# Query norms ahead of unit edges, weight parts behind the first scores, an early Ln/Exp set, and one masked matrix in place of two

## The reference

```
# GLA, chunks of 64 tokens, both directions (second one on flipped tokens), 4 heads, DK=128, DV=256
att = where(lower_tri, q_dec @ k_inv.T, 0)            # 64 x 64 per chunk
o   = att @ v + q_dec @ s
s   = exp(total)[:, None] * s + k_end.T @ v
out = rms_norm(o_fwd + o_bwd) * silu(r)

# attention: 8 query heads, 2 key/value heads, HEAD_DIM=128; layer 0 with context queries, layer 1 without
q, k = rms_norm(q) * g_q, rms_norm(k) * g_k           # rope on latent tokens only
ctx queries read ctx keys (256); latent queries read all keys (512)
o = softmax(q @ k.T / sqrt(128)) @ v

# RG-LRU input: depthwise conv of 4 taps on p[9], evaluated as the projection leaves the accumulators
```

## Time and profile before

| | us |
|---|---|
| median of 3 runs | 2046.06 (2041.23 to 2046.12) |
| profiled execution, its own time | 2039.92 |
| its span | 2038.2 |
| TensorE busy | 1945.4 (95%) |
| VectorE busy | 1164.4 (57%) |
| ScalarE busy | 1002.7 (49%) |
| mean granted TensorE clock | 0.985 of full |
| HBM traffic | 242.21 MB read, 119 GB/s |

### The profile page before, as it was taken

How to read it: one execution, slowest core, us unless ns; L and a number is a source line. 1 busy time by engine, 2 the same in 40 slices (tenths; PEclk the granted TensorE clock), 3 DMA queues, 4 the chain that set the end, 5 groups by cost and what they waited for, 6 DMA issues and landing times.

```text
span 2038.2 us, 26205 instructions
## 1 busy us (share of the span) xinstructions
PE 1945.4 (95%) x10784; PEld 1578.9 (77%) x10784; DVE 1164.4 (57%) x1622; ACT 1002.7 (49%) x1413; POOL 24.3 (1%) x57
## 2 busy tenths in 40 slices
PE   5999999999999999899999999799898999989998
PEld 3788777777777768577766787688687888989997
DVE  3565445545555334765555433766555678668874
ACT  4533346545654223543333333644355688566663
POOL 2000000000000000000000000000000000000000
PEclk9999999999999999899999999899999999999999
DMA  8211111122233554145454533121222354545553
GB/s 310 66 55 53 57 55 60 62 78 93 93 95 103 186 183 148 52 135 199 163 198 163 176 104 106 52 73 55 75 84 72 125 161 147 173 145 166 185 180 122
DMA packets 67990, 244.96 MB, mean 120 GB/s; under 512 B 7696, under 2 KB 8736, under 8 KB 67872
## 3 DMA queue, kind: packets, MB, share of 16 engines
q1 hardware_dynamic: 64736, 232.81, 34.6%
q0 software_dynamic: 1696, 5.24, 0.8%
q10 hardware_dynamic: 1440, 5.24, 0.7%
HBM read 242.21 MB, written 1.05 MB: 119 GB/s over the span
## 4 chain that ended last, share of the span: by engine, by line
PE 73%; DVE 15%; ACT 5%; DMA 3%; issue 3%; SPq 0%; ACTq 0%; DVEq 0%
PE ps L1454 52%; PE ps L1444 4%; DVE wlo L833 4%; PE ps L1389 3%; DVE fa L862 2%; DMA wada<-in_w_ada 2%; ACT whi L438 2%; PE ps L1489 2%; PE ps L1706 2%; PE ps L1796 2%; PE ps L1727 1%; DVE state L1177 1%; DMA wraw<-in_weights 1%; PE ps L1620 1%; PE ps L1630 1%
## 5 line engine op out<-in xcount | busy, mean ns | idle before, releaser
L833 DVE TENSOR_TENSOR wlo<-wraw,whi 128x1024 fp32r<-128x1024 f32 x352 | 429.5, 1223 | 403.4 <-ACT whi L438 402.5
L438 ACT ACTIVATE whi<-wraw 128x1024 fp32r<-128x1024 f32 x352 | 371.4, 1056 | 377.9 <-PE ps L1454 193.7
L1454 PE MATMUL ps<-hh,whi 128*128 128x512 f32 (+1 forms) x1664 | 381.2, 351 | 1.9 <-ACT l_ti L772 1.8
L1454 PE MATMUL ps<-hl,whi 128*128 128x512 f32 (+1 forms) x1664 | 375.0, 348 | 0.0
L1454 PE MATMUL ps<-hh,wlo 128*128 128x512 f32 (+1 forms) x1664 | 344.0, 348 | 1.9 <-DVE wlo L833 1.9
L1454 PEld LDWEIGHTS ps<-hh,whi 128*128 128x128 f32 x1664 | 274.5, 191 | 58.7 <-issue 22.6
L1454 PEld LDWEIGHTS ps<-hl,whi 128*128 128x128 f32 x1664 | 277.1, 191 | 40.2 <-issue 3.6
L1454 PEld LDWEIGHTS ps<-hh,wlo 128*128 128x128 f32 x1664 | 269.6, 190 | 40.4 <-issue 3.0
L862 DVE SCALAR_TENSOR_TENSOR fa<-ps,par,fa 128x510 f32<-128x510 f32 (+1 forms) x176 | 100.1, 610 | 27.8 <-ACT fa L516 26.2
L1454 PE MATMUL ps<-bh,whi 128*128 128x512 f32 (+1 forms) x384 | 89.3, 354 | 0.0
L1454 PE MATMUL ps<-bl,whi 128*128 128x512 f32 (+1 forms) x384 | 82.2, 336 | 0.0
(11 more groups left out here) (285 smaller groups left out, 2556.6 us busy)
## 6 DMA issues: line engine op xcount, KB each, us to landing
wraw<-in_weights SPq DMA_DIRECT2D x352, 512.0 KB, 3.5
wada<-in_w_ada SPq DMA_DIRECT2D x80, 512.0 KB, 5.0
ada_first<-in_w_ada ACTq DMA_DIRECT2D x10, 512.0 KB, 16.6
wgate<-in_w_gate POOLq DMA_DIRECT2D x16, 256.0 KB, 2.8
ada_first<-in_w_ada SPq DMA_DIRECT2D x6, 512.0 KB, 23.9
x<-in_xt SPq DMA_DIRECT2D x4, 512.0 KB, 9.9
out_x<-x SPq DMA_DIRECT2D x4, 256.0 KB, 2.2
par<-in_params POOLq DMA_DIRECT2D x1, 370.0 KB, 8.0
```

Of the source, the lines that this page charges most:

```text
L438: A_(whi[u % HI][:], wraw[RING_W[u] % RAW][:], ACT.Copy).then_inc(s_hi, 1)
L833: V.tensor_tensor(wlo[s][:], wraw[s][:], whi[u % HI][:].bitcast(F32), ALU.subtract).then_inc(s_lo, 1)
L1454: ins = mm(dst[:, r, c:], w[:, kk, r * P:(r + 1) * P], x_[:, UK * h + kk, c:], start=h == 0 and k in (0, 2) and kk == 0, stop=h == m - 1 a ...
```

## The change

Four things. First, in the GLA the 128x128 products are made as 64x64 pieces on the diagonal of the tile only, at two positions of the array. Behind the two masked copies, VectorE adds `attm[:, 0]` and `attm[:, 1]` into a new tile `atts`, and `gla_out` multiplies `atts` once per tile, where it multiplied both. The statistics tile `gstat` moves to memory of its own, since `atts` takes its place. Second, silu of an `r` pair is followed by a load of the set with Ln and Exp. Third, on ScalarE and VectorE the query's square, roots and norm come ahead of edges: the square ahead of the edge for every even head but 0, the roots and the norm ahead of the edge for odd heads too. Fourth, on TensorE: the wait for the last GLA norm stands behind the first two of four sums of squares; one part fewer stands ahead of the swaps; one part of `ua` and two of `ub` stand behind the first scores, and all of ub's later parts shift by two, up to the last one.

```diff
                 elif name == "r":
                     A_(pair_[:, :, c0:], pair_[:, :, c0:], ACT.Silu).then_inc(s_rs, 1)
+                    act.preload_act_table_set(LN_EXP)
...
                         if k == first:
-                            if even:
+                            if h == 0:
                                 edge(v)
                             if h + 2 < AQ:
                                 tile_square(AKV + h + 2)
+                            if even and h:
+                                edge(v)
                         elif not even:
                             edge(v + 1)
                         out_hi(k)
                         if k == first:
-                            if not even:
-                                edge(v)
                             if h + 2 < AQ:
                                 tile_rstd(AKV + h + 2, 7)
-                            if even:
-                                edge(v + 1)
+                            edge(v + 1 if even else v)
...
+                    link(ins)
+                    V.tensor_tensor(atts[:, 0, c0:], attm[:, 0, c0:], attm[:, 1, c0:], ALU.add).then_inc(s_attm, 1)
...
                         if k == first:
-                            if not even:
-                                edge(v)
                             if h + 2 < AQ:
                                 tile_norm(AKV + h + 2)
-                            if even:
-                                edge(v + 1)
+                            edge(v + 1 if even else v)
...
                         for t in range(t_first, TOK // P):
-                            c = slice(t * P, (t + 1) * P)
-                            ins = mm(ps[:, 4 + d, c], gl_ki[:, d, c], gl_qd[:, d, c], start=True, stop=True)
+                            for j in range(2):
+                                c = slice(t * P + j * CHUNK, t * P + (j + 1) * CHUNK)
+                                ins = mm(ps[j * CHUNK:(j + 1) * CHUNK, 4 + d, c], gl_ki[:, d, c], gl_qd[:, d, c], start=True,
+                                         stop=True, tile_position=(0, j * CHUNK))
...
                     for t in range(t_first, TOK // P):
-                        for d in range(2):
-                            mm(ps[:, 4 + t // 2, DV * (t % 2):DV * (t % 2 + 1)], attm[:, d, t * P:(t + 1) * P], gv[:, t, vals],
-                               start=d == 0 and t % 2 == 0, stop=False, skip_group_check=True)
+                        mm(ps[:, 4 + t // 2, DV * (t % 2):DV * (t % 2 + 1)], atts[:, 0, t * P:(t + 1) * P], gv[:, t, vals],
+                           start=t % 2 == 0, stop=False, skip_group_check=True)
...
-                pe.wait_ge(s_on, HEADS * (l + 1))
                 for t in range(4):
+                    if t == 2:
+                        pe.wait_ge(s_on, HEADS * (l + 1))
                     tile_stat(t, 4 + t)
                     parts(ua, 2 + t, 3 + t)
-                parts(ua, 6, 8)
+                parts(ua, 6, 7)
                 for t in range(4):
                     pe.wait_ge(s_aln, A_TILES * l + t + 1)
                     tile_swap(t, 4 + t)
-                    parts(ua, 8 + t, 9 + t)
+                    parts(ua, 7 + t, 8 + t)
                 wait_pair_taken(pe, l, "akv", 1)
                 pe.wait_ge(s_arope, A_TILES * l + 4)
                 scores(0)
+                parts(ua, 11, 12)
+                parts(ub, 0, 2)
                 for h in range(AQ):
-                    b = 15 * h
+                    b = 15 * h + 2
```

More of the change, by code:

```diff
@@ L151, in build @@
         one, eps = sb("one", [P, 1]), sb("eps", [P, 1])
+        gstat = sb("gstat", [P, 2, TOK // P])
         mx = sb("mx", [P, 4, 2])
@@ L199, in build @@
         lr = at("lr", M + 49, [2 * LRP, TOK])
-        gstat = at("gstat", M + 50, [P, 2, TOK // P])
+        atts = tiles("atts", M + 50, 1)
         prob = [tiles(f"prob{i}", M + 8 + 2 * i, 2) for i in range(2)]
@@ L1159, in mask_att @@
                     for d in range(2):
-                        V.copy_predicated(attm[:, d].rearrange("p (t c) -> p t c", c=P)[:, v],
-                                          KEEP[:, d:d + 1].broadcast_to([P, (TOK - c0) // P, P]),
-                                          ps[:, 4 + d].rearrange("p (t c) -> p t c", c=P)[:, v]).then_inc(s_attm, 1)
+                        ins = V.copy_predicated(attm[:, d].rearrange("p (t c) -> p t c", c=P)[:, v],
+                                                KEEP[:, d:d + 1].broadcast_to([P, (TOK - c0) // P, P]),
+                                                ps[:, 4 + d].rearrange("p (t c) -> p t c", c=P)[:, v])
+                    link(ins)
+                    V.tensor_tensor(atts[:, 0, c0:], attm[:, 0, c0:], attm[:, 1, c0:], ALU.add).then_inc(s_attm, 1)
                 def states(h, e):
@@ L1615, in gla_out @@
                         pe.wait_ge(s_gm, n + 2)
[L1616 removed]
+                    pe.wait_ge(s_attm, n + 1)
                     vals = slice(DV * h, DV * (h + 1))
                     for t in range(t_first, TOK // P):
[L1619 to L1621 removed]
+                        mm(ps[:, 4 + t // 2, DV * (t % 2):DV * (t % 2 + 1)], atts[:, 0, t * P:(t + 1) * P], gv[:, t, vals],
+                           start=t % 2 == 0, stop=False, skip_group_check=True)
                     pe.wait_ge(s_state, n * 4 + 4)
@@ L1668, in _ @@
                     parts(u, 5, 8)
-                    pe.wait_ge(s_attm, (h + HEADS * l) * 2 + 2)
+                    pe.wait_ge(s_attm, h + HEADS * l + 1)
                     if h < HEADS - 1:
@@ L1768, in _ @@
                             tile_swap(AKV + h + 2, 7)
-                        parts(ub, b + 13, b + 15)
+                        parts(ub, b + 13, min(b + 15, 15 * AQ))
                     else:
@@ L1782, in _ @@
                             tile_swap(AKV + h + 2, 7)
-                        parts(ub, b + 11, b + 15)
+                        parts(ub, b + 11, min(b + 15, 15 * AQ))
                 def lru_gates(n):
```

## The result

The changed kernel takes 2011.67 us (median of 4 runs; the lowest 2010.39) against 2045.05 for the kernel before in the same comparison: a ratio of 0.9838, 95% interval 0.982 to 0.9856. One of the four runs, at 10769.87 us, is a disturbed one and no part of the ratio; the other three have a median of 2010.85. In three later comparisons, on three chips, the same kernel before had medians of 2040.39, 2040.68 and 2040.75; in the second of them the changed kernel, word for word, took 2012.45: 0.9855 (0.9839 to 0.9872). So the change is worth 28 to 33 us, of which some 5 us stand on what the kernel before does in one session or another.

The account below looks back on a forecast made before the run. TensorE, busy 1945.4 of 2038.2 us, was taken as the bound. -10.7 + 0.3 - 8.2 - 4.3 = -22.9 us took the profiled 2039.92 to 2017.0, carried over to the median 2023.2 us; range 2013 to 2034.

Parts of the forecast that it names:

- the base: Whole kernel: the profiled run lay 6.1 us under the median of 2046.06; carrying that over turned 2017.0 into 2023.2.
- the pieces: GLA's masked matrices in 64x64 pieces: 32 loads of 54 ns take 1.72 us, as before; +0.3 us.
- the clock: TensorE's clock drops behind attention stalls: 2.5 of five go, 1.7 us each, -4.3 us; bounds 0 and -8.5.
- the stalls: TensorE's waits in both layers' attention: 22.6 us become 14.4 (4.8 in layer 0, 9.6 in layer 1), -8.2 us.
- the first squares: Layer 0 attention, wait for the last GLA norm: 1.95 us stall behind 2.4 us of work, 0.4 left.
- the second scores: Attention, three parts now in front: layer 0's 2.13 us wait goes, layer 1's 3.09 becomes 1.65.
- The matmuls: GLA product of the merged masked matrices: half its matmuls go, 7.1 us in layer 0, 3.6 in layer 1, -10.7 us.
- The addition on VectorE: GLA, adding the two masked copies: 0.7 us, done 2.2 us before TensorE needs it, so worth nothing.
- B: Rival, GLA: the 64x64 pieces overlap, the stretch halves, 5 us more gain, 2018 us; chance 0.17.
- C: Rival, GLA pieces: an instruction costs the same whatever its size, +10.2 us, 2033 us in all; chance 0.11.
- D: Rival, attention: stalls only move, six of eight us return, five clock drops stay; whole change 12.4, 2034 us; chance 0.12.
- E: Rival, attention, slower: PSUM pairs freed late cost 4.5 us each; eight of 16 give +13, 2059 us; chance 0.04.

Follow-up runs that it names:

- the repeats: The changed kernel and the kernel before, each run again word for word with its own profile: 2012.45 us median, and 2042.12 us in one execution.
- the grouped run: Changed kernel with its 64x64 pieces ordered by array position instead of alternating: 2017.1 us, against 2040.39 for the kernel before.
- the other engines' order alone: Kernel before with only the new order of squares, roots and norms on ScalarE and VectorE, no early set: 2039.41 us against 2040.68, 0.999.

## Why the prediction was wrong, point by point

The forecast of 2023.2 is 11.5 us above 2011.67, and 2011.67 is 1.3 us outside the range. The miss has two halves and four terms: the base (4.8), the pieces (2.9), the clock (2.3) and the stalls (2.1). Each of them alone is larger than the 1.3 us.

**The base, 4.8 us.** "carried over to the median": I added the 6.1 us by which the profiled run lay under the median of three. The changed kernel's profiled run lies 1.3 us under its median. This step failed: the distance between the profiled run and the median belonged to those three runs, and the changed kernel doesn't have it. In 31 later runs on three chips the kernel before has 2039.18 to 2043.77, so the profiled 2039.92 was an ordinary value and the 2046 of two of those three runs the odd one. Why the first comparison has 2041.23 to 2046.12 for it is open. Against 2040.7 the same −22.9 gives 2017.8, and the measured 28.2 us of the later comparison is 5.3 more than I said.

**The change, 6.6 us** (−29.5 between the two profiled runs, 2039.92 and 2010.39, where I had −22.9):

- **The pieces, 2.9 us.** "32 loads of 54 ns are 1.72 us, as now": this step failed. 1.08 us were measured, and 2.6 us is what the pieces are worth in all, where I had +0.3. The rival that I gave 0.17, pieces at two positions overlap, was the right mechanism with half its price: 34 ns a record, neither 54 nor 27. The row of the state product said so, and I let a difference of two load durations overrule it; the loads overlap more when their positions differ, as the grouped run shows. The Trainium skill, "TensorEngine Tiling (Array Packing)", Key Properties, says of the tiles that they load and multiply in parallel; the two runs agree, 1.08 against 1.83 us.
- **The clock, 2.3 us.** Attention columns −16.9, stalls −10.3, so −6.6 is the clock's, where I had −4.3. The windows agree: 8.5 us lost before, 1.7 after. My 2.5 drops of five was a guess between bounds, and the repeats show the measured figure to be one draw among several: with the second profiles it is 8.6 to 3.4, 5.2 us.
- **The stalls, 2.1 us.** −10.3 for −8.2. In layer 0 I had 4.8 and 4.78 was measured, with each of the three left where I had put it (1.2, 1.2, 2.0 for 1.31, 1.46, 2.01). That the sum agrees so well is part luck: the 0.4 that I left at the first squares was wrong by my own figures (2.4 us of work cover a stall of 1.95) and didn't come, and the others came out as much higher. In layer 1 I had 9.6 for 7.57: the wait moved from the swap to the part behind the conv in head 3, 2.8 for 2.42, the second scores 1.65 for 1.67, the first 2.0 for 1.61, head 5 1.1 for 0.80; the sums of squares 1.4 for 1.07; the 0.3 each at heads 0 and 7 didn't come.
- **The matmuls, right.** −10.7; whole tiles, which keep the merge and drop the pieces, shorten the GLA columns by 6.93 + 3.56 = 10.5. The addition on VectorE was hidden, as said.
- **Elsewhere**, +0.80, +1.04 and −1.42: no part of the change. The stretch behind the attention is 418.9 to 419.0 in ten of thirteen profiles, the second one of the kernel before among them, 420.4 in two, the first one of before one of them, and 417.5 in one. Why was not tried.

The rivals: B is the pieces' bullet. C (an instruction costs the same at any size) is out, 34 ns. D (stalls only move) is out for the whole and true for one part: the other engines' order alone gave 1.3 us. E (pairs freed late) happened once, in head 3, and I had counted it.

## What to carry to other kernels

Matmuls on half the array's columns pay when neighbours alternate between the halves; ordered by position they can cost more than whole ones, so read both from a row of the same kernel before adding load times. A move that lets work past a long instruction must be followed to the next consumer behind that instruction (norm, then rope), and needs filler work on the bounding engine where that one waits. Take a base from many runs: a median of three can be off by more than the terms that one argues about. Price the clock by the us lost over several profiles: a count of drops hides that one may last twice as long.

## What the runs showed of the hardware

- Whether a stall of TensorE costs a drop of its clock differs between executions of the same kernel: 2.01 us of idle time at the same instruction once kept 1.00 and once had 0.83 over 10 us. In the attention a low stretch is at half the full clock (0.50, the lower of the two levels) for 3.4 us, which is 1.7 us of full speed lost, or in some profiles once for twice that (3.4 us lost, from 1534 in the second profile of before). The losses of one profile are one draw.
- Records of the 64x64 pieces start 34 ns apart with alternating positions and 57 ns apart at one position; the whole ones 107 ns apart. A load of 64 columns lasts 137 ns in either order; 192 of them are 6.3 us of busy time alternating and 10.4 grouped.
- A set that holds both Ln and Exp saves the load between the two: 1.28 us each, and the instruction behind a load starts as it ends, here too (1505.57 + 1.28, Ln at 1506.87).
